# A fused two-block kernel: another order of the side work in the chunk stage, and the rwkv output inside it

## What is computed

```python
proj = h @ w_in
o_pool = causal_pool_mixer(pool_u, pool_w, pool_scale) * silu(pool_g)
o_ret = retention(q, k, v, positions, ret_norm_g) * silu(ret_g)
o_rwkv = rwkv7_time_mix(rw, ...) * silu(rw_g)
branches = stack([o_pool, o_ret, o_rwkv], axis=2)
y = einsum('btnw,nwd->btnd', branches, w_branch)
gates = sigmoid(gate_logits.reshape(B, T, 3, D))
merged = sum(gates * y, axis=2)
return x + gate * (merged @ w_out)
```

## Time and profile before

| | |
|---|---|
| median of 3 runs | 3694.54 us (3694.33 to 3698.45) |
| profiled execution | 3703.0 us |
| its span | 3701.2 us |
| granted TensorE clock, mean | 0.964 |
| PE busy | 3465.2 us (94% of the span) |
| PE weight loads | 2810.1 us (76%) |
| DVE busy | 1703.6 us (46%) |
| ACT busy | 1124.8 us (30%) |
| POOL busy | 192.5 us (5%) |
| PE share of the chain that ended last | 59% (DVE 8%, ACT 2%) |
| chunk stage, layer 0 and layer 1 | about 312 to 795 us and 1128 to 1600 us |

### The profile page before, as it was taken

One profiled execution on the slowest core, in us unless ns is written; L12 is line 12 of the kernel. 1 busy time (PEld: TensorE's weight loads), 2 busy tenths in 40 slices (PEclk: granted clock), 3 DMA queues, 4 the chain that ended last, 5 costly groups with the idle time before them and its releaser, 6 DMA issues.

```text
span 3701.2 us, 43137 instructions
## 1 busy us (share of the span) xinstructions
PE 3465.2 (94%) x17128; PEld 2810.1 (76%) x17128; DVE 1703.6 (46%) x2431; ACT 1124.8 (30%) x1645; POOL 192.5 (5%) x222
## 2 busy tenths in 40 slices
PE   8999999988999999999999988999999998879999
PEld 7777778767777778778888756888888886568887
DVE  2644553455644553354332675433343336653333
ACT  2532323333432232223321333322133213333221
POOL 1000000000000000000000210000000002000000
PEclk8999999999999999999999979999999999789999
DMA  4221212223221111122232201223222322012232
GB/s 178 80 74 63 69 59 84 69 103 106 74 75 62 59 46 52 52 103 87 101 108 91 74 29 52 103 97 108 80 97 101 106 84 80 29 63 97 97 109 74
DMA packets 83513, 303.17 MB, mean 82 GB/s; under 512 B 9696, under 2 KB 9968, under 8 KB 83312
## 3 DMA queue, kind: packets, MB, share of 16 engines
q1 hardware_dynamic: 77920, 282.59, 21.9%
q0 software_dynamic: 5392, 17.83, 1.4%
HBM read 295.66 MB, written 4.72 MB: 81 GB/s over the span
## 4 chain that ended last, share of the span: by engine, by line
PE 59%; DVE 8%; ACT 2%; issue 1%; POOL 1%; DMA 0%; DVEq 0%; POOLq 0%; ACTq 0%; SPq 0%
PE bank L530 18%; PE bank L532 17%; PE bank L531 17%; PE bank L881 2%; PE bank L536 2%; DVE acc L1150 2%; DVE wlo L1144 1%; DVE xn L1150 1%; PE bank L1103 1%; PE bank L1127 1%; ACT pr L1960 1%; DVE G L1144 1%; DVE hl L1144 0%; DVE U L1144 0%; DVE pr L1920 0%
## 5 line engine op out<-in xcount | busy, mean ns | idle before, releaser
L530 PE MATMUL bank<-hh,whi 128*128 128x512 f32 (+1 forms) x2704 | 1088.9, 403 | 55.1 <-DVE mrg L1144 12.6
L532 PE MATMUL bank<-hh,wlo 128*128 128x512 f32 (+1 forms) x2704 | 1041.5, 385 | 0.0
L531 PE MATMUL bank<-hl,whi 128*128 128x512 f32 (+1 forms) x2704 | 1041.2, 385 | 0.0
L1144 DVE TENSOR_TENSOR wlo<-raw,whi 128x1024 fp32r<-128x1024 f32 x498 | 610.5, 1226 | 819.5 <-ACT whi L1965 777.8
L1965 ACT CAST whi<-raw 128x1024 fp32r<-128x1024 f32 x514 | 539.9, 1050 | 790.7 <-PE bank L532 734.8
L530 PEld LDWEIGHTS bank<-hh,whi 128*128 128x128 f32 x2704 | 523.7, 194 | 194.5 <-issue 69.2
L532 PEld LDWEIGHTS bank<-hh,wlo 128*128 128x128 f32 x2704 | 522.9, 193 | 100.2
L531 PEld LDWEIGHTS bank<-hl,whi 128*128 128x128 f32 x2704 | 524.8, 194 | 80.9 <-issue 1.9
L530 PE MATMUL bank<-whi,fh 128*128 128x512 f32 x704 | 279.7, 397 | 0.0
L532 PE MATMUL bank<-whi,fl 128*128 128x512 f32 x704 | 279.2, 397 | 0.0
L531 PE MATMUL bank<-wlo,fh 128*128 128x512 f32 x704 | 279.1, 396 | 0.0
(11 more groups left out here) (324 smaller groups left out, 3859.7 us busy)
## 6 DMA issues: line engine op xcount, KB each, us to landing
raw<-in_W SPq DMA_DIRECT2D x514, 512.0 KB, 3.2
bc<-in_ln_g POOLq DMA_DIRECT2D x6, 512.0 KB, 4.3
bc<-in_ln_b POOLq DMA_DIRECT2D x6, 512.0 KB, 5.8
xn<-in_x SPq DMA_DIRECT2D x4, 512.0 KB, 7.2
AR<-in_W SPq DMA_DIRECT2D x2, 1024.0 KB, 11.1
mrg<-in_W SPq DMA_DIRECT2D x2, 1024.0 KB, 12.9
xn<-in_x POOLq DMA_DIRECT2D x4, 512.0 KB, 5.0
xd<-xn POOLq DMA_DIRECT2D x4, 512.0 KB, 3.6
```

Of the source, the lines that this page charges most:

```text
L530: e.matmul(out, ah, bh, start=first, stop=False, skip_group_check=True)
L531: e.matmul(out, ah, bl, start=False, stop=False, skip_group_check=True)
L532: return e.matmul(out, al, bh, start=False, stop=last, skip_group_check=True)
L1144: return self.e.tensor_tensor(o, a, b, op)
```

## The change

1. The side work's order is `retention`, `branch(l, 1, 2)`, `out_gates`, `last_gates`, in all four classes.
2. `chunks` has 6 more steps: 4 empty ones ahead of the last `tail` and 3 instead of 1 between `tail` and `tail_end`. The mix runs over 192 main steps and makes 14 side steps fewer (331 and 307).
3. On DVE and ACT the side steps that are left over are no longer drained alone: `rwkv_out` has become a generator and its parts are put between them, by `mix(side, self.rwkv_out(l), 14, 4)`. On PE and POOL they are drained as before.

```diff
+LAST = 14
@@ Lane.chunks
         for c in range(4):
             for g in range(2):
                 yield from self.chunk(l, c, g)
+        for _ in range(4):
+            yield
         self.tail(l, 3, 1)
-        yield
+        for _ in range(3):
+            yield
         self.tail_end(l, 3, 1)
         yield
@@ layer_a of TensorE and Pool
         side = itertools.chain(self.retained(l), weave(itertools.chain(
-            self.retention(l), self.last_gates(l), self.branch(l, 1, 2), self.out_gates(l)), self.adas_of(l), 8))
-        mix(self.chunks(l), side, 186, SIDE[l])
+            self.retention(l), self.branch(l, 1, 2), self.out_gates(l), self.last_gates(l)), self.adas_of(l), 8))
+        mix(self.chunks(l), side, 192, SIDE[l] - LAST)
         drain(side)
@@ layer_a of VectorE and ScalarE (VectorE has mod_columns before rwkv_out)
-            self.retention(l), self.last_gates(l), self.branch(l, 1, 2), self.out_gates(l)), self.adas_of(l), 8))
+            self.retention(l), self.branch(l, 1, 2), self.out_gates(l), self.last_gates(l)), self.adas_of(l), 8))
         self.paced = True
-        mix(self.chunks(l), side, 186, SIDE[l])
-        drain(side)
+        mix(self.chunks(l), side, 192, SIDE[l] - LAST)
+        mix(side, self.rwkv_out(l), LAST, 4)
         self.paced = False
         self.at(("out", l))
-        self.rwkv_out(l)
@@ VectorE.rwkv_out
             if p:
                 self.lower(HALF(k.ol, p - 1), HALF(k.KH, p - 1), HALF(k.oh, p - 1), ...)
+            if p < 3:
+                yield
         self.lower(HALF(k.ol, 3), HALF(k.KH, 3), HALF(k.oh, 3), [("oh", l, 2, 3)], [("ol", l, 2, 3)])
```

## The result

| | before | changed |
|---|---|---|
| median | 3694.61 us (4 runs, 3694.33 to 3698.45) | 3719.52 us (4 runs, 3717.92 to 3723.80) |
| ratio | | 1.0067, 95% interval 1.0049 to 1.0084 |
| profiled execution, its span | 3703.0, 3701.2 us | 3718.7, 3716.9 us |
| granted clock, mean | 0.964 | 0.958 |

The change costs 25 us. The forecast was 10 us less, and the time lies above the range. In later comparisons the kernel before took 3696.5 to 3698.3 us, so times from different comparisons can be some 4 us apart for no reason of the kernels. One execution of e3 took 4321.05 us at a granted clock of 0.742 and is left out of its time.

The account below looks back on a forecast made before the run. PE, busy 94% of the span, was taken as the bound, so only its idle time and clock could be won. -24.3 + 0.95 + 9.0 + 2 + 2 + 0.5 = -9.9 us gave 3684.6 us, range 3673 to 3694.

Parts of the forecast that it names:

- Gains at the ends: PE's stalls at the last chunk's tail and ahead of branch 2, both layers, would go, clock included: -24.3 us.
- the 1 us on bank 0: Start of branch 2, layer 0: PE must wait for the last out gate's sigmoid in the same bank, +0.95 us.
- New wait elsewhere at the ends: Layer 1's start of branch 2, POOL's x load, SP's fetches and the weight units' order: no new wait.
- Less cover in the chunk stage: Fewer side steps per chunk step make PE's waits in the chunk stage grow: +9.0 us, ends +3 and +22.
- The clock: Longer waits in the chunk stage may put more time at the lower granted clock: +2 us, ends -4 and +7.
- Out gates inside the stage: Out gates now run between chunk steps and queue on DVE ahead of the chunk's U: +2 us, ends 0 and +10.
- Branch 1 right behind retention: Branch 1's k = 3 step may wait for the last head's oh and ol: +0.5 us both layers, ends 0 and +3.
- rival 4: DVE's order decides: each out gate holds DVE ahead of a U in the chunk stage; +11 us, 3706, chance 0.06.
- rival 1: Cover is nearly free: chunk waits and clock stay and out_gates hide; -20 us, 3674, chance 0.15.

Follow-up runs that it names:

- e3: The kernel before with only the new order of the side work; ratio, tail and rwkv_out as before: 3692.0 us, ratio 0.9985.
- h1: The changed kernel with 334 and 303 side steps mixed over the 192 main steps, instead of 331 and 307: 3681.39 us, ratio 0.9960.
- g4: e2 with seven idle DVE operations put between G and U in the last three chunks of each layer: 3714.11 us, ratio 1.0042.
- g5: e2 with the same seven idle DVE operations in the fourth level of the last three chunks of each layer: 3685.22 us, ratio 0.9964.
- k1: The changed kernel, with DVE's blocks of branch 1 put off four side steps where they would fall on bad places: 3705.40 us, ratio 1.0026.
- g3: The changed kernel with 362 and 334 side steps over 192, the count with least DVE block time at bad places: 3660.82 us, ratio 0.9900.
- g1: The changed kernel with 314 and 314 side steps mixed over the 192 main steps: 3705.23 us, ratio 1.0021.
- k2: g3 with DVE's blocks of branch 1 put off four side steps where they would fall on bad places: 3658.00 us, ratio 0.9893.
- e2: The changed kernel with 355 and 331 side steps over 192, giving back about the ratios of the kernel before: 3683.11 us, ratio 0.9963.
- g2: The changed kernel with 339 and 338 side steps mixed over the 192 main steps: 3715.37 us, ratio 1.0051.

## Why the prediction was wrong

Step by step, as it was put:

- **Gains at the ends**: 24.3 less 0.95 forecast, 22.1 measured. Right, the 1 us on bank 0 included (0.84). Left over: a YN wait of 1.05 in layer 1, where 0.2 was allowed.
- **New wait elsewhere at the ends**: none, as said.
- **"Less cover in the chunk stage", +9.0**: this step failed, and with it the forecast. This term and the three small ones were to be 13.5 us for the stages; they cost 45.0. The working of the cover term compared the waits of the two layers at two ratios and took the difference for a price of cover. But the two ratios also put other pieces of DVE's side work at the tight places of the chunks, and where they fall moves the time far more than the ratio does: h1 takes 38 us off at constant cover, g4 shows waits one for one with a block at the start, g5 none mid chunk, k1 gives 14 us for four blocks moved. Of the waits that grew, U, SP and X were named (KH grew in layer 0 and shrank in layer 1); G, up by 6.2 us in layer 1, was not named. A forecast had to lay the side work out against the chunk steps for the new ratio; the mix formula and DVE's durations were all there. That alone would not have given the size: at the 1.1 us for each microsecond that was fitted ahead of g3, the count's growth from 23.9 to 40.2 is an estimate of 18 us of the 45, less than the 22.1 that the ends gained.
- **The clock, +2, ends -4 and +7**: the second failure. The stages lost 23.8 us more to it. In the changed kernel the granted clock fell to its lower level 15 times in the two stretches, 11 times behind or within a single wait of 1.45 to 3.87 us, the other four behind shorter waits or none; in the kernel before it fell 9 times, 4 of them at the ends. The term was made from one stretch, not from a count of such waits.
- **Out gates inside the stage, +2**: not borne out as such. e3 has them there and is not slower. The mechanism behind that term, DVE's fixed order, was the right one with the wrong actors: branch 1's block (2.9 us), rope (2.8) and weight subtractions (1.2), not the gates' single multiplies. The Trainium skill ("TensorE: Matmul & The Clock Gate", "Architectural detail") calls VectorE strict FIFO; the rows of chunk 5 agree, U standing 2.9 us behind side work for which PE did not wait there.
- **Branch 1 right behind retention, +0.5**: no wait of PE for ol is seen there.
- **Rivals**: rival 4, DVE's order, had the right sign (+11 against +25) and 0.06 of the chance; rival 1 (cover nearly free) isn't excluded by h1, but needs other places than the change has. I gave too little to a mechanism of which the earlier trace rows showed a case.

What is shown is that long DVE side work ahead of a chunk's tight link costs its length and more, and that moving it gains. That it accounts for all 45 us is argued, not shown. Whether less cover costs anything at equal places stays open. So does what makes up the 24 us between g1 and h1.

## What to carry to other kernels

Where two streams are merged by a fixed ratio, the cost can be set less by the ratio than by which long piece of the side stream lands on the tight link of the main one. Lay both out before touching the ratio, order or length of either, and move long pieces off the tight link by rule (k2: 40 us less than the kernel before, with the change's order and ends, other counts and one `if`). Count every piece, the short ones too; the count here left the weight subtractions out. A saving at the ends of a stage is to be tested with the inside of the stage held still.

## What the runs showed that I had not expected

- Seven side steps among 638 moved the time by 38 us, 1%.
- A wait of PE costs more than itself: g4's 19.6 us of added waits came with 11.9 us at the lower clock, the changed kernel's stages lost 23.8 us more to the clock and 20.8 to idle time.
- The stretch ahead of the chunk stage is the same in e2 and g2, yet took from 301.9 (e2) to 311.9 us (g2) in the profiled executions. Single executions are therefore compared by stretches, and totals by medians.
